# The layer norm's weight and bias on the kept token rows: from VectorE's program to GpSimd's

## The reference

```python
for l in range(2):
    x = layer_norm(ALPHA * x + token_mixing(x, ...), ln1_g[l], ln1_b[l])
    x = layer_norm(ALPHA * x + conv_ffn(x, ...), ln2_g[l], ln2_b[l])

def layer_norm(x, g, b):
    mu, var = mean(x), mean(square(x - mu))          # over the 1024 columns, per token
    return (x - mu) * rsqrt(var + 1e-5) * g + b
```

## Time and profile before

| | us |
|---|---|
| median of 3 runs | 3657.33 (3655.13 to 3659.92) |
| the profiled execution | 3652.21 |
| its span | 3650.2 |
| TensorE busy | 3537.4 |
| VectorE busy | 2049.0 |
| ScalarE busy | 1433.9 |
| GpSimd busy | 169.8 |

### The profile page before, as it was taken

How to read it: one execution, slowest core, us unless ns; L and a number is a source line. 1 busy time by engine, 2 the same in 40 slices (tenths; PEclk the granted TensorE clock), 3 DMA queues, 4 the chain that set the end, 5 groups by cost and what they waited for, 6 DMA issues and landing times.

```text
span 3650.2 us, 48825 instructions
## 1 busy us (share of the span) xinstructions
PE 3537.4 (97%) x19264; PEld 2829.6 (78%) x19264; DVE 2049.0 (56%) x3633; ACT 1433.9 (39%) x2222; POOL 169.8 (5%) x277
## 2 busy tenths in 40 slices
PE   8999999999999999999999989999999899989999
PEld 7777677887777767778776867788888788868887
DVE  5756766777757566677886645422232544463333
ACT  3556634442325566343323354321212355542222
POOL 0000000000001000000001300100000221100000
PEclk9999999999999999999999999999999999999999
DMA  4121233334431222434353100112121211112322
GB/s 180 65 83 68 87 134 114 139 116 175 144 121 65 76 76 83 149 106 156 133 179 136 55 22 13 58 41 87 39 83 44 96 53 65 44 55 83 107 95 85
DMA packets 66085, 338.62 MB, mean 93 GB/s; under 512 B 6848, under 2 KB 8384, under 8 KB 40512
## 3 DMA queue, kind: packets, MB, share of 16 engines
q1 hardware_dynamic: 65856, 335.51, 26.2%
HBM read 327.09 MB, written 8.39 MB: 92 GB/s over the span
## 4 chain that ended last, share of the span: by engine, by line
PE 82%; DVE 11%; ACT 5%; issue 1%; POOL 1%; DMA 0%; DVEq 0%; ACTq 0%; POOLq 0%; SPq 0%
PE ps L2004 24%; PE ps L2006 23%; PE ps L2005 23%; PE ps L1993 4%; PE ps L2145 3%; PE ps L2013 3%; DVE wl L2277 3%; DVE ha L2285 1%; DVE junk L2322 1%; ACT wh L2164 1%; DVE tt L2285 1%; PE ps L2020 1%; DVE hl L2285 1%; ACT epb L2265 0%; DVE gs L2277 0%
## 5 line engine op out<-in xcount | busy, mean ns | idle before, releaser
L2164 ACT ACTIVATE wh<-raw 128x2048 fp32r<-128x2048 f32 (+4 forms) x279 | 458.0, 1642 | 728.8 <-PE ps L2006 724.6
L2277 DVE TENSOR_TENSOR wl<-raw,wh 128x2048 fp32r<-128x2048 f32 (+4 forms) x279 | 546.0, 1957 | 329.5 <-ACT wh L2164 310.0
L2004 PE MATMUL ps<-hh,wh 128*128 128x512 f32 (+1 forms) x1184 | 430.0, 363 | 13.5 <-DVE hl L2285 10.4
L2005 PE MATMUL ps<-hl,wh 128*128 128x512 f32 (+1 forms) x1184 | 422.7, 357 | 0.0
L2006 PE MATMUL ps<-hh,wl 128*128 128x512 f32 (+1 forms) x1184 | 422.4, 357 | 0.0
L2004 PE MATMUL ps<-xhb,wh 128*128 128x512 f32 x848 | 369.9, 436 | 11.2 <-DVE xlb L2277 10.4
L2006 PE MATMUL ps<-xhb,wl 128*128 128x512 f32 x848 | 337.1, 397 | 0.0
L2005 PE MATMUL ps<-xlb,wh 128*128 128x512 f32 x848 | 336.8, 397 | 0.0
L2004 PE MATMUL ps<-xha,wh 128*128 128x512 f32 x704 | 280.4, 398 | 8.9 <-DVE xla L2277 4.4
L2005 PE MATMUL ps<-xla,wh 128*128 128x512 f32 x704 | 278.7, 396 | 0.0
L2006 PE MATMUL ps<-xha,wl 128*128 128x512 f32 x704 | 278.7, 396 | 0.0
(11 more groups left out here) (326 smaller groups left out, 6802.3 us busy)
## 6 DMA issues: line engine op xcount, KB each, us to landing
raw<-in_wts SPq DMA_DIRECT2D x196, 1024.0 KB, 4.8
lt<-in_wts SPq DMA_DIRECT2D x110, 512.0 KB, 3.5
raw<-in_wts SPq DMA_DIRECT2D x44, 512.0 KB, 3.5
raw<-in_wts SPq DMA_DIRECT2D x28, 448.0 KB, 3.2
x_scratch<-xt SPq DMA_DIRECT2D x3, 2048.0 KB, 11.6
xt<-x_scratch SPq DMA_DIRECT2D x3, 2048.0 KB, 8.0
oe<-in_relb SPq DMA_DIRECT2D x16, 384.0 KB, 3.7
raw<-in_wts SPq DMA_DIRECT2D x4, 768.0 KB, 4.1
```

The costliest lines, as they stand in the source:

```text
L2004: T.matmul(u.out, u.sh, u.mh, start=u.first, stop=False)
L2005: T.matmul(u.out, u.sh, u.ml, start=False, stop=False)
L2164: A.activation(u.h, u.raw, ACT.Copy).then_inc(*act.inc())
L2277: V.tensor_tensor(o_, a, b, op).then_inc(*dve.inc())
```

## The change

The branch for `ln_gain` leaves `dve_program` and stands, with the same waits, in `pool_program`. What waited for VectorE's last unit of a norm (the release of both panels and the store) waits for GpSimd's. The order of the units is unchanged.

```diff
@@ -1258,9 +1258,9 @@
                     def gain(i=i):
                         u = add("ln_gain", x=XT[:, i, :], g=pg.v[:, 0, :], b=pb_.v[:, 0, :], g_t=pg.w, b_t=pb_.w, came=turned_t[7])
                         if i == 3:
-                            pg.done(DVE(u))
-                            pb_.done(DVE(u))
-                            add("load", dst=xkeep.rearrange("(i p) n -> p i n", p=P), src=XT[:, :, :], sem=s_xd, free=[DVE(u)])
+                            pg.done(POOL(u))
+                            pb_.done(POOL(u))
+                            add("load", dst=xkeep.rearrange("(i p) n -> p i n", p=P), src=XT[:, :, :], sem=s_xd, free=[POOL(u)])
                             nxd[0] += 1
                             stored[0] = (s_xd, 16 * nxd[0])
                     later(small, 20 + 16 * i, gain)
@@ -2431,12 +2431,6 @@
-                elif kind == "ln_gain":
-                    dve.wait_ge(*u.g_t)
-                    dve.wait_ge(*at(u.came))
-                    tt(u.x, u.x, u.g, ALU.mult)
-                    dve.wait_ge(*u.b_t)
-                    tt(u.x, u.x, u.b, ALU.add)
@@ -2582,6 +2576,12 @@
+                elif kind == "ln_gain":
+                    pool.wait_ge(*u.g_t)
+                    pool.wait_ge(*at(u.came))
+                    tt(u.x, u.x, u.g, ALU.mult)
+                    pool.wait_ge(*u.b_t)
+                    tt(u.x, u.x, u.b, ALU.add)
```

## The result

The changed kernel takes 3664.34 us (median of 20 runs, 3660.17 to 3668.90), the kernel before 3657.42 us in the same comparison (20 runs, 3652.91 to 3661.69). The ratio is 1.0021 with a 95% interval of 1.0015 to 1.0027: slower by 5.5 to 9.9 us. The forecast was 3664.5.

The account below looks back on a forecast made before the run. TensorE was taken to bound the kernel, busy for 97% of the span. Two feed-forward stages at 2.2 us plus 2.8 in the mixing stage made +7.2 us on the 3657.3 median, 3664.5; range 3651 to 3673.

Parts of the forecast that it names:

- VectorE's relief: Mixing stage of layer 1: moving units off VectorE shortens four chains behind TensorE's gaps, gaining 7.6 to 8.6 us if nothing is added.
- One burst from the fence on: GpSimd after each of three norms: eight instructions run directly behind the fence, 19 us, about 24 with waits.
- 2.35 us per instruction: GpSimd: time of one moved unit instruction of width 1024, given as 2.3 to 2.4 us.
- The reads are held: SBUF: a GpSimd unit instruction blocks VectorE's two-operand SBUF reads for 2.04 of its 2.35 us; reads with PSUM operands go free.
- Feed-forward stages: Two stages: held reads delay wl, stalling TensorE 1.2 and 1.0 us, 2.2 per stage, 4.4 together.
- Mixing stage: Layer 1: held rotation reads cost more than the relief returns, +2.1 or +3.5 us by order, taken as +2.8.
- With wl first: Mixing stage, VectorE's wl reads before the burst: TensorE gaps 2.29, 4.58 and 0.53, 7.4 us against 5.31, +2.1.
- With GpSimd first: Mixing stage, the burst reads before wl: TensorE gaps 1.95, 0.90 and 5.98, 8.8 us against 5.31, +3.5.
- The clock: Mixing stage: granted-clock losses follow two long gaps before and after the change and cancel, so they add nothing.
- Rival (a): Both engines' SBUF reads go side by side, only the relief is left: 3649 us, faster; chance 0.14.
- Rival (b): Reads held for the whole 2.35 us: 3.9 per feed-forward stage, 4.6 to 5.6 in mixing, +12.9, 3670; chance 0.16.
- Rival (c): VectorE mostly reads first: feed-forward stages cost about 1 each, mixing gains 2, 3657, no change; chance 0.06.

## Why the prediction was right, step by step

- **VectorE's relief, 7.6 to 8.6 us, all in the mixing stage.** Right: 7.7 us by the medians with the units left out (ratio 0.9981), 8.6 in that trace, 9.2 in the trace with the units nine steps later, and nothing in the feed-forward stages.
- **One burst from the fence on.** Right in all three places; 25.1 us long where "about 24" was said.
- **2.35 us per instruction.** Measured 2.38.
- **The reads are held from 0.14 after the start to 0.17 before the end, 2.04 us.** The first ha of the burst ended at 629.17, and the GpSimd instruction behind it (started at 628.70) ended 2.27 us later, at 631.44, so it asks 2.38 - 2.27 = 0.11 after its start. gl ended at 631.98 and needs 0.69: it read from 631.29, 0.15 before that end. Held for 2.12 us; 0.08 more than forecast.
- **Feed-forward stages: gaps of 1.2 and 1.0, 2.2 per stage.** Right in mechanism and place: idle times of 1.16 and 1.10, 1.15 and 1.10. They end at 636.5 and 649.0; the prediction's 633.6 and 646.0, moved by the 1.4 us that this execution is late and by the gap itself, give 636.2 and 648.4. But the prediction worked with start times, and in starts the cost is 1.42 and 1.36, 2.8 per stage in place of 2.2. This term was too small, though inside the 1.6 to 3.6 given for it. The longer hold is a part of it: wl of panel 2 ended at 636.40, by before's clock 635.0 in place of 634.76.
- **Mixing stage, +2.8 us.** The mechanism held, the size did not. With wl first the gaps forecast were 2.29, 4.58 and 0.53; they were 1.92, 4.32 and none, 6.24 against 7.4. In place of +2.8 the trace shows +1.2 us over the stage. This term was too large by 1.6. With GpSimd first (the run with four units moved) 1.62, 2.50 and 4.35, 8.5 against a forecast of 8.8, and +3.9 us over the stage against +3.5. Both orders occur; whether the runs of the change without a profile hold a mixture of them is not shown.
- **The clock.** None of the new feed-forward gaps of 1.1 us is followed by a lower granted clock; in the mixing stage the losses did not quite cancel. The busy times of the stretches of the earlier trace rows (the clock is the third column from the end), then the stretches at the lower level in the mixing stage, two of the change and two of before:

```profile
625.00:675.00 50.00, 47.74 (x204) 37.77 (x203) 36.04 (x31) 21.78 (x23) 21.21 (x8) 1.00 0.33 116
1011.00:1064.00 53.00, 46.76 (x190) 34.70 (x190) 32.79 (x30) 13.27 (x14) 19.93 (x7) 0.90 0.20 72
...
1015.10:1018.40 3.30, 3.30 (x7) 1.96 (x6) 1.79 (x1) 1.43 (x1) 3.22 (x2) 0.50 0.00 0
1025.40:1032.10 6.70, 4.67 (x9) 3.05 (x10) 5.20 (x5) 0.60 (x1) 5.84 (x3) 0.50 0.00 1
...
1019.10:1022.40 3.30, 3.30 (x9) 2.56 (x8) 1.71 (x4) 0.01 (x1) 0.00 (x0) 0.50 0.00 0
1036.20:1039.50 3.30, 3.30 (x10) 2.52 (x9) 1.01 (x2) 0.21 (x1) 0.00 (x0) 0.50 0.00 0
```

  TensorE's 50.00 of the feed-forward stretch have become 47.74 at a clock of 1.00: the 2.26 us of the two gaps. The matmuls in it fell from 216 to 204, and twelve at 0.23 us are the 2.8 us of delay. In the mixing stage TensorE worked at half speed for 3.3 + 4.7 us in place of 3.3 + 3.3, by estimate from these rows 0.7 us more lost. With 0.93 us more idle time that is 1.6; two stops fewer (four gaps have become two) give back some 0.5 by the 0.26 us that a gap of the feed-forward stage hides. That comes near the 1.2 measured.
- **Rival (a), reads side by side,** is refuted by the durations and by the run without reads, which shows what (a) would have brought. **Rival (b), the whole hold,** forecast 3.9 us per feed-forward stage; 2.8 is measured, and the reads are held for 2.12 of 2.38 us. **Rival (c)** forecast 3657; the interval excludes it.

Sum of the trace: 2.8 + 2.8 + 1.2 = 6.8 us, where the comparison of medians has 6.9. The forecast's 7.2 is nearly the same total from other parts: the feed-forward stages were 1.2 us too small together, the mixing stage 1.6 too large, although a clock loss of about 0.7 that the forecast had put at nothing came on top there. The mechanism was right, but that 3664.5 met 3664.34 so closely is luck.

## What to carry to other kernels

An idle engine is not a free one: where VectorE and GpSimd both read two operands in SBUF, each waits for nearly the whole of the other's instruction (2.12 of 2.38 us here), so work moved over should be cut into short instructions (in the feed-forward stages 256 and 512 columns cost TensorE nothing, 1024 cost 2.8 us a stage) or placed beside work that reads PSUM. A lag that places a unit in one engine's program places it in no other: in a program with nothing else to do the units run as soon as their waits allow, here in the first 25 us of the stage. When the chain runs through movable work, try its place before its engine: nine steps later on VectorE gave all of the 8 us. And a forecast that adds up several stages is checked stage by stage in the trace, since a right total can hide errors that cancel.

## What was not expected of the hardware

GpSimd pays as well: its median instruction took 2.74 us and its longest 4.35 in place of 2.38, since it waits until wl is done. And pieces are cheaper for VectorE than their count suggests: four of 256 columns at 0.74 us take 2.96 us in place of 2.38, and the burst 36 us in place of 25, yet the longer burst costs TensorE nothing in the feed-forward stages.
